# Three attentions: softmax sums leave TensorE, are inverted for four blocks at once and come back as rows through DRAM; GpSimd scales and gates the results

## What is computed

```python
# first block: three dilated bands, weighted by their log sums; the kernel
# computes them as one masked attention over all 1024 keys
o = jnp.einsum('bhrnqk,bhrnke->bhrnqe', p, vw) / den[..., None]
...
wts = jax.nn.softmax(jnp.stack(lses), axis=0)
return jnp.sum(wts[..., None] * jnp.stack(outs), axis=0)

# second block: plain attention, 2 key heads for 8 query heads, then a gate
p = jax.nn.softmax(scores, axis=-1).astype(v.dtype)
return jnp.einsum('bkgqs,bskd->bqkgd', p, v)
...
y_attn = _attention(q, k, v) * jax.nn.silu(g_a)
```

## Time and profile before

| | us |
|---|---|
| median of 3 runs | 3846.07 (3844.93 to 3848.85) |
| the profiled execution | 3854.1 |
| its span | 3852.3 |
| TensorE busy | 3479.2 (90%) |
| VectorE busy | 1898.8 (49%) |
| ScalarE busy | 1327.7 (34%) |
| POOL busy | 148.9 (4%), all of it starting DMAs |

### The profile page before, as it was taken

The page is one execution under the profiler, slowest core; times in us unless marked ns, Lnnn a source line. Parts: engine busy times, 40 slices in busy tenths (PEclk is TensorE's granted clock), DMA queues, the critical chain, the costliest instruction groups (busy, mean ns, idle before and its releaser), DMA issues.

```text
span 3852.3 us, 40354 instructions
## 1 busy us (share of the span) xinstructions
PE 3479.2 (90%) x16662; PEld 2818.3 (73%) x16662; DVE 1898.8 (49%) x2479; ACT 1327.7 (34%) x1866; POOL 148.9 (4%) x261
## 2 busy tenths in 40 slices
PE   5999999988897599989999998889799978988987
PEld 3888888866875488768888886568588745867874
DVE  6233333366427699353333334641498465137963
ACT  4111111145121288231111112531288164216843
POOL 0000000000100111000000000010100001000000
PEclk8999999999996699999999999999899989988998
DMA  5222222212742344112222221132411103332111
GB/s 193 92 84 71 82 73 78 74 67 104 174 145 81 77 73 70 56 66 82 88 75 73 83 82 44 46 112 82 124 28 33 56 1 100 112 101 67 28 39 44
DMA packets 130838, 304.44 MB, mean 79 GB/s; under 512 B 32456, under 2 KB 80364, under 8 KB 119648
## 3 DMA queue, kind: packets, MB, share of 16 engines
q1 hardware_dynamic: 69104, 204.74, 15.3%
q0 software_dynamic: 61552, 97.12, 10.5%
HBM read 249.73 MB, written 52.09 MB: 78 GB/s over the span
## 4 chain that ended last, share of the span: by engine, by line
PE 78%; DVE 12%; ACT 5%; issue 3%; DMA 2%; SPq 0%; POOL 0%; ACTq 0%; DVEq 0%; POOLq 0%
PE psum L603 56%; PE psum L871 4%; PE psum L894 4%; PE psum L861 4%; PE psum L630 2%; PE psum L947 1%; PE psum L882 1%; DVE h_lo L1509 1%; PE psum L701 1%; PE psum L937 1%; DVE w_lo L1459 1%; DMA fo_alt<-in_alternating 1%; PE psum L795 1%; ACT attn_num L1301 1%; DVE p_u L1596 1%
## 5 line engine op out<-in xcount | busy, mean ns | idle before, releaser
L603 PE MATMUL psum<-h_hi,w_hi 128*128 128x512 f32 x2112 | 833.6, 395 | 45.3 <-DVE h_lo L1509 27.2
L603 PE MATMUL psum<-h_lo,w_hi 128*128 128x512 f32 x2112 | 825.2, 391 | 0.0
L603 PE MATMUL psum<-h_hi,w_lo 128*128 128x512 f32 x2112 | 825.1, 391 | 0.0
L603 PEld LDWEIGHTS psum<-h_hi,w_hi 128*128 128x128 f32 x2112 | 398.5, 189 | 142.9 <-issue 46.0
L603 PEld LDWEIGHTS psum<-h_hi,w_lo 128*128 128x128 f32 x2112 | 398.5, 189 | 83.6
L603 PEld LDWEIGHTS psum<-h_lo,w_hi 128*128 128x128 f32 x2112 | 398.9, 189 | 82.7 <-issue 2.7
L1060 ACT ACTIVATE w_hi<-w_raw 128x2048 fp32r<-128x2048 f32 (+2 forms) x135 | 226.2, 1675 | 556.7 <-PE psum L603 468.1
L1459 DVE TENSOR_TENSOR w_lo<-w_raw,w_hi 128x2048 fp32r<-128x2048 f32 (+2 forms) x135 | 269.4, 1995 | 248.9 <-ACT w_hi L1060 248.2
L1558 DVE TENSOR_TENSOR gate<-gate,psum 128x1024 f32<-128x1024 f32 x44 | 53.7, 1221 | 608.1 <-PE psum L603 608.1
L603 PE MATMUL psum<-a_hi,w_hi 128*128 128x512 f32 x704 | 274.1, 389 | 3.4 <-DVE a_lo L1560 3.4
L603 PE MATMUL psum<-a_lo,w_hi 128*128 128x512 f32 x704 | 273.9, 389 | 0.0
(11 more groups left out here) (352 smaller groups left out, 5341.2 us busy)
## 6 DMA issues: line engine op xcount, KB each, us to landing
w_raw<-in_w_ada SPq DMA_DIRECT2D x52, 1024.0 KB, 5.0
...
w_raw<-in_w_down SPq DMA_DIRECT2D x24, 512.0 KB, 3.5
...
qk_hi_scratch<-p_out_hi POOLq DMA_DIRECT2D x18, 512.0 KB, 3.0
qk_lo_scratch<-p_out_lo POOLq DMA_DIRECT2D x18, 512.0 KB, 3.8
```

The source lines that it names most:

```text
L603: mm = e.matmul(p.half[h], a[:, k * width + m * P:k * width + (m + 1) * P], b(k)[:, h * HALF:(h + 1) * HALF], start=(k == order[0] and i = ...
```

## The change

- `spread_sum`, `diagonal` and the reciprocal of each block go. The exponential accumulates its sum into column u of a 128x64 tile `sums`. Every four blocks VectorE inverts four columns at once (`inverse_sums`, group z).
- SP, which gets a list of its own for the attentions, writes these 512 numbers to DRAM (in runs of 4 bytes, since they lie across partitions), waits, and reads them back as a row, broadcast to 64 partitions (`rs`).
- The result of four blocks now fills a whole PSUM bank. ScalarE copies the upper half (64x512) and VectorE adds it to the lower one, straight into `og`, unscaled. There are two `og` tiles in turn.
- GpSimd multiplies each 64x512 part by its row and, after every fourth group of the gated attentions, the 128x1024 tile by its gate. The gate tiles are now loaded by SP.
- High and low parts of a head pair are made five blocks later than the pair's last sum, apart from each other (`heads_high` behind step 24 + 16k, `heads_low` behind step 25 + 16k).
- In attn1 the queries' gain and the band change sign. The row minimum of the negated scores is then the bias as it stands, the exponential takes scale -1, and the 128x1 multiplication goes.
- The band is loaded by SP into a weight buffer (`w_raw`) right after SP's part of the mLSTM. The next weight block for this buffer (the third of the output product) is loaded after the last masked maximum. In the gated attentions the third output block is likewise loaded after SP's attention list.

Of the removed functions (`spread_sum`, `diagonal`, the old `half_result` and `results`) little is shown here; they stand in the listing above.

```diff
-        a.sm = rings(f"{name}_sm", 2, [P, 4], F32, scope)
-        a.dg = [t.sqh[1][:, (i + 1) * P:(i + 2) * P] for i in range(3)]
-        a.ones = t.sqh[1][:, 0:P]
-        a.tm = [t.sqh[0][0:64, i * 256:(i + 1) * 256] for i in range(2)]
-        a.og = sb(f"{name}_o", [P, S], F32, scope)
+        a.sm = rings(f"{name}_sm", 2, [P, 1], F32, scope)
+        a.sums = sb(f"{name}_sums", [P, A_HEADS * ST], F32, scope)
+        a.inv = sb(f"{name}_inv", [P, A_HEADS * ST], F32, scope)
+        a.tm = [t.sqh[i][0:64, :] for i in range(2)]
+        a.rs = rings(f"{name}_rows", 2, [P, HALF], F32, scope)
+        a.og = [sb(f"{name}_o", [P, S], F32, scope), t.acc if between else sb(f"{name}_o1", [P, S], F32, scope)]
         return a
...
+    first_out1 = next(n for n, entry in enumerate(plan) if entry[3] == ("out1", 0))
+    t.mix1.at.mask = t.raw[first_out1 % RAW][:, 0:1920]
...
-            def spread_sum(u):
...
-                kv = kv_of(hd)
+                kv, z = kv_of(hd), w // 2
                 if part == 0:
                     e.wait_ge(*num_lo.at(name, 2 * w + 1, 1))
                     if i == 0 and (hd == 0 or kv != kv_of(hd - 1)):
                         e.wait_ge(*v_in[kv % 2].at(name, kv))
+                    if w % 2 == 0 and z >= 2:
+                        e.wait_ge(*res_done.at(name, z - 2))
                 for j in range(ST):
-                    mm = e.matmul(p_o.half[w % 2][:, 0:256], a.v[kv % 2][:, j, :], (a.th, a.tl)[part][w % 2][:, j, :],
-                                  start=(part == 0 and j == 0), stop=(part == 1 and j == ST - 1))
+                    mm = e.matmul(p_o.half[z % 2][:, (w % 2) * 256:(w % 2 + 1) * 256], a.v[kv % 2][:, j, :],
+                                  (a.th, a.tl)[part][w % 2][:, j, :], start=(part == 0 and j == 0),
+                                  stop=(part == 1 and j == ST - 1))
                 if part == 1:
...
-            for u in range(n + 4):
+            for u in range(n + 3):
                 if u < n:
                     scores(u)
-                if 1 <= u <= n:
+                if 1 <= u < n + 1:
                     turn_over(u - 1)
-                if u >= 3 and u % 2 == 1 and u < n + 3:
-                    spread_sum(u - 3)
-                    spread_sum(u - 2)
-                    times_v((u - 3) // 2, 0)
-                if u >= 4 and u % 2 == 0:
-                    times_v((u - 4) // 2, 1)
+                if u >= 3:
+                    times_v((u - 3) // 2, 1 - u % 2)
             here("PE", mix)
...
+            def half_result(z):
+                e.wait_ge(*pv_done.at(name, 2 * z + 1))
+                if z >= 2:
+                    e.wait_ge(*res_done.at(name, z - 2))
+                e.activation(a.tm[z % 2], ps.of[(name, "o")].half[z % 2][64:128, :], ACT.Identity).then_inc(*half_res.mark(name, z))
+            def heads_high(pp):
+                e.wait_ge(*(og_scaled.at(name, 4 * pp + 3) if masked else og_gated.at(name, pp)))
+                e.activation(mixa[0][:, pp, :], a.og[pp % 2][:], ACT.Identity).then_inc(*mix_hi.mark(mix, "a", pp))
...
-                if u >= 2:
+                if not masked and u >= 2:
                     e.wait_ge(*num_turned.at(name, u - 2, 1))
-                e.activation(s[:], s[:] if masked else ps.of[(name, "s", u % 2)].full, ACT.Exp, bias=m[:, 1:2],
-                             accum_out=m[:, 2:3]).then_inc(*exped.mark(name, u))
-            def diagonal(u):
...
-            for u in range(n + 4):
-                if u >= 5 and u % 2 == 1:
-                    half_result((u - 5) // 2)
-                if 1 <= u <= n:
+                e.activation(s[:], s[:] if masked else ps.of[(name, "s", u % 2)].full, ACT.Exp, bias=m[:],
+                             scale=-1.0 if masked else 1.0, accum_out=a.sums[:, u:u + 1]).then_inc(*exped.mark(name, u))
+            for u in range(n + 9):
+                if u >= 7 and (u - 7) % 4 == 0 and u < n + 7:
+                    half_result((u - 7) // 4)
+                if 1 <= u < n + 1:
                     num_high(u - 1)
                 if u < n:
                     numerators(u)
-                if 1 <= u <= n:
-                    diagonal(u - 1)
+                if u >= 24 and (u - 24) % 16 == 0:
+                    heads_high((u - 24) // 16)
...
-            e.tensor_scalar(cols[:, 16:17], vc("g_q"), A_DIM ** -0.5, None, ALU.mult).then_inc(*norm.mark("gain q"))
+            e.tensor_scalar(cols[:, 16:17], vc("g_q"), -A_DIM ** -0.5, None, ALU.mult).then_inc(*norm.mark("gain q"))
...
-                    e.tensor_tensor_reduce(out=s[:], in0=p.full, in1=a.mask[:, o:o + S], scale=1.0, scalar=-3e38, op0=ALU.add,
-                                           op1=ALU.max, accum_out=m[:, 0:1]).then_inc(*maxed.mark(name, "raw", u))
-                    e.wait_ge(*maxed.now())
-                    e.tensor_scalar(m[:, 1:2], m[:, 0:1], -1.0, None, ALU.mult).then_inc(*maxed.mark(name, u))
+                    e.tensor_tensor_reduce(out=s[:], in0=p.full, in1=a.mask[:, o:o + S], scale=1.0, scalar=3e38, op0=ALU.add,
+                                           op1=ALU.min, accum_out=m[:]).then_inc(*maxed.mark(name, "raw", u))
+                    maxed.value[(name, u)] = maxed.count
                 else:
-                    e.tensor_reduce(m[:, 1:2], p.full, AX.X, ALU.max, negate=True).then_inc(*maxed.mark(name, u))
+                    e.tensor_reduce(m[:], p.full, AX.X, ALU.max, negate=True).then_inc(*maxed.mark(name, u))
...
+            def inverse_sums(z):
+                e.wait_ge(*exped.at(name, 4 * z + 3))
+                e.reciprocal(a.inv[:, 4 * z:4 * z + 4], a.sums[:, 4 * z:4 * z + 4]).then_inc(*recip.mark(name, z))
+            def results(z):
+                hh, pp = (z // 2) % 2, z // 4
+                e.wait_ge(*half_res.at(name, z))
+                if z % 4 == 0 and pp >= 2:
+                    e.wait_ge(*mix_lo.at(mix, "a", pp - 2))
+                e.tensor_tensor(a.og[pp % 2][64 * hh:64 * hh + 64, (z % 2) * HALF:(z % 2 + 1) * HALF],
+                                ps.of[(name, "o")].half[z % 2][0:64, :], a.tm[z % 2], ALU.add).then_inc(*res_done.mark(name, z))
+            def heads_low(pp):
+                e.wait_ge(*mix_hi.at(mix, "a", pp))
+                e.tensor_tensor(mixa[1][:, pp, :], a.og[pp % 2][:], mixa[0][:, pp, :].bitcast(F32),
+                                ALU.subtract).then_inc(*mix_lo.mark(mix, "a", pp))
+            for u in range(n + 10):
                 if u < n:
                     maximum(u)
-                if u >= 5 and u % 2 == 1:
-                    results((u - 5) // 2)
-                if 1 <= u <= n:
+                if u >= 7 and (u - 7) % 4 == 0 and u < n + 7:
+                    results((u - 7) // 4)
+                if 1 <= u < n + 1:
                     low_parts(u - 1)
-                    e.wait_ge(*exped.at(name, u - 1))
-                    e.reciprocal(a.sm[(u - 1) % 2][:, 3:4], a.sm[(u - 1) % 2][:, 2:3]).then_inc(*recip.mark(name, u - 1))
+                if u >= 4 and u % 4 == 0 and u <= n:
+                    inverse_sums(u // 4 - 1)
+                if u >= 25 and (u - 25) % 16 == 0:
+                    heads_low((u - 25) // 16)
...
-        def attention(name, a, n_kv, gates_from):
+        def attention(name, a, n_kv, gated):
             n = A_HEADS * ST
-            e.dma_start(a.ones, ins["mats"][MAT["ones"]]).then_inc(*at_const.mark(name))
             load_kv(name, a, 1)
-            for u in range(n + 4):
+            for u in range(n + 8):
                 if u < n and u % ST == ST - 1 and u // ST + 2 < A_HEADS:
                     load_q(name, a, u // ST + 2)
-                w = (u - 3) // 2
-                if u >= 3 and u % 2 == 1 and u < n + 3 and w % ST == 0 and gates_from is not None:
-                    pp = w // ST
-                    if pp:
-                        e.wait_ge(*mix_lo.at(gates_from[1], "a", pp - 1))
-                    e.dma_start(a.g[:], d.proj[gates_from[0] + pp]).then_inc(*at_gate.mark(name, pp))
-                w = (u - 4) // 2
-                if n_kv == A_HEADS and u >= 4 and u % 2 == 0 and w % (ST // 2) == ST // 2 - 1 and w // (ST // 2) + 2 < n_kv:
-                    load_kv(name, a, w // (ST // 2) + 2)
+                if u >= 8 and u % 4 == 0:
+                    z = u // 4 - 2
+                    hh, pp = (z // 2) % 2, z // 4
+                    part = a.og[pp % 2][64 * hh:64 * hh + 64, (z % 2) * HALF:(z % 2 + 1) * HALF]
+                    e.wait_ge(*res_done.at(name, z))
+                    e.wait_ge(*inv_in[z % 2].at(name, z))
+                    e.tensor_tensor(part, part, a.rs[z % 2][64 * hh:64 * hh + 64, :], ALU.mult).then_inc(*og_scaled.mark(name, z))
+                    if gated and z % 4 == 3:
+                        e.wait_ge(*at_gate.at(name, pp))
+                        e.wait_ge(*og_scaled.now())
+                        e.tensor_tensor(a.og[pp % 2][:], a.og[pp % 2][:], a.g[:], ALU.mult).then_inc(*og_gated.mark(name, pp))
```

(41 more changed lines are left out.)

60 lines of the change are left out of this document (9 added, 51 removed).

## The result

The changed kernel takes 3862.55 us (3860.98 to 3867.54, 6 runs) against 3848.28 of the kernel before beside it: ratio 1.0042, interval [1.0031, 1.0053]. It is slower by some 14 us. Forecast were 3802 us, range 3780 to 3830. The profiled executions' spans are 3865.7 and 3852.3, so the trace has 13.4 us to explain, where the forecast had -44.2.

What follows compares the result with a forecast made beforehand. Outside the attentions TensorE bounds; inside, a ScalarE-TensorE circle of 2.87 us and TensorE's queue, late in every second block. Loops -58.3, start of attn1 -3.3, tails +17.4 give -44.2 us: 3802 us, range 3780 to 3830.

Steps and rivals of the forecast that it cites:

- Row sums off TensorE: Attention loops: TensorE's queue falls to 2.76 us per block, leaving the 2.87 us circle through ScalarE and TensorE as pace.
- Results every four blocks: Attention loops: one VectorE 64x512 sum per four blocks, charged 0.15 us for each of 15 blocks, 2.3 us per attention.
- Ends of heads: Ends of head pairs: ScalarE's 2.79 us wait goes; remaining work charged 0.9 us, three times, 2.7 per attention.
- Sum of a loop: First to last exponential: attn2 187.3 us for 207.5, twice; attn1 189.2 for 207.1; together -58.3 us.
- Tail of each attention: After the last low part: first mix high part later by 5.0 us (attn1), 6.2 (attn2, twice); together +17.4 us.
- (a): Tail: last inverse sums go to DRAM and back, 3.0 us each way plus 0.3 for reciprocal and issue.
- (b): Tail: GpSimd's products taken at twice VectorE's time, 1.3 us for 512 columns and 2.5 for 1024.
- Inside the loops the same round trip is covered: Attention loops: inverse sums leave at step 4z+4, their sum is ready at 4z+7, its high part wanted five steps later.
- The round trip is slow, the tails take all: Rival, tails: +36 us in place of +17 with slow 4-byte runs; about 3820 us; chance 0.10.
- The slower rival: Rival, SP's queue: trip with product over 13 us puts GpSimd behind in every group; 3906 us; chance 0.05.
- VectorE paces: Rival, loops: maximum, low parts and new sums in VectorE's one queue cost in full; 3832 us; chance 0.11.
- GpSimd and VectorE block each other: Rival, loops: low parts of head pairs (12 times) and GpSimd's products wait for each other; 3818 to 3832 us; chance 0.04.

Runs made afterwards that it cites:

- no trip: Changed kernel without storing and reading back the inverse sums, row tiles filled once from a stored projection (wrong scale factors): 3796.33 us, ratio 0.9867.
- 128 runs of 4: Changed kernel storing only the first of a group's four columns, 128 runs of 4 bytes, rows filled from a stored projection: 3827.35 us, ratio 0.995.
- gate loads later: Changed kernel, 4-byte runs kept, with SP loading a pair's gate behind its third group's store: 3858.74 us, ratio 1.0026.
- the turned one: Changed kernel with reciprocals transposed on VectorE in 32x32 pieces, stored as 16 runs of 128 bytes in four DMAs: 3796.79 us, once more 3795.40 us.

## Why the prediction was wrong, step by step

Forecast and trace are 57.6 us apart (-44.2 and +13.4): 38.2 of them in the tails, 20.5 in attn1's loop, nothing else is over 3. Both come from one term, the time of a store of 4-byte runs.

- *Row sums off TensorE*: right in the mechanism. The step is 2.93 us for 2.87 forecast, and apart from the first one or two (3.6 to 3.8) none in attn2 is over 3.3. Of the circle, turn to high part is 0.69 for 0.63 (2876.53 to 2877.22).
- *Results every four blocks*, *Ends of heads*: both charged too much. A step with a new sum takes 2.93 us like the others, so the sums cost nothing for 2.3. A head end costs 0.07 + 0.34 us in two steps (2.99 and 3.27) for 0.9, so 1.2 us for 2.7.
- *Sum of a loop*: 187.1 and 186.5 for 187.3. That it is so near is partly luck: 63 steps of 2.93 for 2.87 cost 3.8 us more, which the two charges above give back. attn1 would have been 188.7 for 189.2 (no trip), but was 209.7.
- *Sign, maximum*: nothing, as said. *Start of attn1*: -5.6 for -3.3, inside its ends of 0 and -6.7; the band left at 1315.94 and took 7.66 us.
- *Tail of each attention*: **wrong, in (a)**. "With 512 runs of 4 bytes I take 3.0 for each way": the store takes 10.2 us, above even the worst end of 6.4, and the read 4.6. On top comes SP's lag of up to 8.6 us, which the sum didn't have. With a store of 2.1 us the tails are 3.9, 5.0 and 5.0 us longer than before, for 5.0, 6.2 and 6.2 forecast. (b) held: 1.28 and 2.39 us for 1.3 and 2.5. They are 1.9 and 2.0 times VectorE's 0.67 and 1.22, so the trace agrees with the 1.96 of the GPSIMD Engine Reference of the Trainium skill, section 3.
- *Inside the loops the same round trip is covered*: **wrong, for the same number.** I set the trip against the five blocks till heads_high, for one group alone. I didn't set SP's occupancy of 10.7 us a group against the 11.7 of four blocks, nor the gate load that it waits for ahead of each pair (49.8 us round against 47.2). The prediction's own sign for this case, over 8 us for a trip, is there: a store and a read take 14.8. Nor did I name what stands behind the waiting product on POOL's queue, though it was the loads of the next head: 21 us in attn1.
- *The round trip is slow, the tails take all* (0.10) comes nearest to the cause, with a price too low: +36 us for the tails, which grew by 55.6, and nothing for attn1's loop.
- *The slower rival* (0.05) was right that SP's queue falls behind, and wrong in price and condition. It put store, read and product in one chain of 13.5 us for each group; they take 16.1, and 16 of them would be 258 us, where the loops of attn2 take 187. SP waits only for the store in each group, and for read, product and gate once in a pair of heads: that circle, which in attn2_0 the chain follows through 13 of its 16 stores, is 2.6 us too long a pair, and it ends in the tail and not in the loop. The bound for a store of short runs was drawn from a row of 512 KB with 2048 runs (6.4 us); no row of the kernel before has runs of single words.
- *VectorE paces* is refuted by the loops. (In attn2_0's loop VectorE was busy 89% before and is so after, ScalarE 84% and 80%; the "over nine tenths" given for both above is too high.) *GpSimd and VectorE block each other* costs the changed kernel nothing: none of the 12 low parts of a head pair runs beside an instruction of GpSimd (1.22 us as before). But the mechanism is there. In two other kernels one of them meets a product, first with 128 runs of 4, then with gate loads later:

```profile
2929.97 1.29 POOL L2189 TENSOR_TENSOR ada_acc<-ada_acc,attn_rows 64x512 f32<-64x512 f32 x1 [11.44 <-DMA attn_rows<-proj_scratch]
2930.61 1.73 DVE L1856 TENSOR_TENSOR mix2a_lo<-attn_o,mix2a_hi 128x1024 fp32r<-128x1024 f32 x1
```

```profile
3672.38 1.27 POOL L2189 TENSOR_TENSOR ada_acc<-ada_acc,attn_rows 64x512 f32<-64x512 f32 x1 [2.04 <-DMA attn_rows<-inverse_sums]
3673.16 1.57 DVE L1856 TENSOR_TENSOR mix2a_lo<-attn_o,mix2a_hi 128x1024 fp32r<-128x1024 f32 x1
```

These two take 1.73 and 1.57 us where all others take 1.21 to 1.23, and both end 1.08 us behind the product's end, as if they had waited for it.

With that one term put right in the kernel, the turned one, 3795.4 us was measured where the forecast said 3802.
